# State-space stage of a two-block network: conditioning rows in one bank, another TensorE order, eight powers of C

## The reference

```python
def adaln(cond, w, b):
    return jnp.split(jax.nn.silu(cond) @ w + b, 6, axis=-1)
def s5_discretise(a_re, a_im, log_dt, b_re, b_im):
    lam = lax.complex(a_re, a_im); dt = jnp.exp(log_dt)[:, None]
    lam_bar = jnp.exp(lam * dt)
    b_bar = ((lam_bar - 1) / lam)[..., None] * b
    return lam_bar, b_bar
def s5_scan(u, lam_bar, b_bar, s0, reverse):
    bu = jnp.einsum('btgh,gph->btgp', u, b_bar)
    first = -1 if reverse else 0
    bu = bu.at[:, first].add(lam_bar * s0)
    a = jnp.broadcast_to(lam_bar, bu.shape)
    _, states = lax.associative_scan(_lin_rec_combine, (a, bu), axis=1, reverse=reverse)
    return states
def s5_mixer(...):
    y_lat = u_lat * d
    for direction in range(2):
        st_ctx = s5_scan(uc_ctx, lam_bar, b_bar, s0, reverse)
        s_ctx_final = st_ctx[:, 0] if reverse else st_ctx[:, -1]
        st_lat = s5_scan(uc_lat, lam_bar, b_bar, s_ctx_final, reverse)
        y_lat = y_lat + jnp.einsum('btgp,ghp->btgh', st_lat, c_mat).real
    z = gelu(y_lat); a, g = jnp.split(z @ w_glu, 2, axis=-1)
    return a * sigmoid(g)
```

## Time and profile before

| | us |
|---|---|
| median of 3 runs | 3676.69 (3676.04 to 3678.21) |
| profiled execution | 3674.07 |
| its span, first to last instruction | 3672.3 |
| PE busy | 3381.4 (92%) |
| DVE, ACT, POOL busy | 2140.5, 1399.7, 500.4 |
| granted clock, mean | 0.939 |
| HBM read | 637.54 MB, 175 GB/s over the span |

### The profile page before, as it was taken

One profiled execution on the slowest core, in us unless ns is written; L12 is line 12 of the kernel. 1 busy time (PEld: TensorE's weight loads), 2 busy tenths in 40 slices (PEclk: granted clock), 3 DMA queues, 4 the chain that ended last, 5 costly groups with the idle time before them and its releaser, 6 DMA issues.

```text
span 3672.3 us, 53215 instructions
## 1 busy us (share of the span) xinstructions
PE 3381.4 (92%) x21377; PEld 2858.0 (78%) x21377; DVE 2140.5 (58%) x1867; ACT 1399.7 (38%) x1409; POOL 500.4 (14%) x339
## 2 busy tenths in 40 slices
PE   3778888979999999897698999999999899999998
PEld 2456667868888888776577888888877788888887
DVE  6337665555565656659855555555563555555555
ACT  3245553443333333332234433433332344344333
POOL 1647780000000000029300000000000000000000
PEclk8678778989999999998889999999999999999999
DMA  7776666535556565443224555555542455555552
GB/s 224 248 258 202 202 207 217 187 96 183 185 181 194 185 192 183 160 138 134 101 94 148 186 191 184 186 190 184 187 153 80 143 189 188 183 189 185 193 183 92
DMA packets 350993, 642.91 MB, mean 175 GB/s; under 512 B 21599, under 2 KB 50359, under 8 KB 350519
## 3 DMA queue, kind: packets, MB, share of 16 engines
q1 hardware_dynamic: 350080, 641.37, 53.1%
q10 hardware_dynamic: 823, 0.29, 0.0%
HBM read 637.54 MB, written 4.06 MB: 175 GB/s over the span
## 4 chain that ended last, share of the span: by engine, by line
PE 86%; DVE 5%; ACT 3%; DMA 3%; issue 2%; DVEq 0%; ACTq 0%; SPq 0%
PE acc L436 48%; PE acc L437 24%; PE acc L1186 2%; ACT u L1435 2%; DMA raw<-in_w_mod_dram 2%; PE acc L1245 2%; PE acc L1216 1%; DVE z L912 1%; DVE w_lo L758 1%; PE acc L1292 1%; PE acc L1280 1%; PE acc L1262 1%; PE acc L1231 1%; PE acc L516 1%; PE acc L528 1%
## 5 line engine op out<-in xcount | busy, mean ns | idle before, releaser
L436 PE MATMUL acc<-xin,w_hi 128*128 128x512 f32 x5376 | 1912.1, 399 | 58.0 <-DVE xin L772 33.7
L758 DVE TENSOR_TENSOR w_lo<-raw,w_hi 128x2048 fp32r<-128x2048 f32 x488 | 1120.1, 2301 | 1079.3 <-ACT w_hi L612 1078.9
L437 PE MATMUL acc<-xin,w_lo 128*128 128x256 f32 x5376 | 1519.1, 283 | 0.0
L612 ACT ACTIVATE w_hi<-raw 128x2048 fp32r<-128x2048 f32 x488 | 934.3, 1918 | 1365.4 <-PE acc L437 1364.3
L436 PEld LDWEIGHTS acc<-xin,w_hi 128*128 128x128 f32 x5376 | 1017.5, 189 | 309.9 <-issue 35.9
L437 PEld LDWEIGHTS acc<-xin,w_lo 128*128 128x128 f32 x5376 | 1021.4, 190 | 0.0
L436 PE MATMUL acc<-hid,w_hi 128*128 128x512 f32 x2432 | 845.4, 392 | 0.0
L437 PE MATMUL acc<-hid,w_lo 128*128 128x256 f32 x2432 | 681.2, 280 | 0.0
L436 PEld LDWEIGHTS acc<-hid,w_hi 128*128 128x128 f32 x2432 | 455.1, 187 | 101.3
L437 PEld LDWEIGHTS acc<-hid,w_lo 128*128 128x128 f32 x2432 | 459.6, 189 | 0.0
L764 DVE TENSOR_REDUCE tmp<-acc 128x1024 f32<-128x2048 f32 x116 | 264.9, 2284 | 19.9 <-PE acc L437 19.9
(11 more groups left out here) (237 smaller groups left out, 2286.1 us busy)
## 6 DMA issues: line engine op xcount, KB each, us to landing
raw<-in_w_mod_dram SPq DMA_DIRECT2D x96, 1024.0 KB, 9.2
raw<-in_ffn_w_gate_dram SPq DMA_DIRECT2D x88, 1024.0 KB, 5.2
raw<-in_ffn_w_up_dram SPq DMA_DIRECT2D x88, 1024.0 KB, 5.2
raw<-in_ffn_w_down_dram SPq DMA_DIRECT2D x88, 1024.0 KB, 5.1
raw<-in_w_mlp_in_dram SPq DMA_DIRECT2D x64, 1024.0 KB, 5.3
raw<-in_w_mlp_out_dram SPq DMA_DIRECT2D x64, 1024.0 KB, 5.1
raw<-in_s_w_glu_dram SPq DMA_DIRECT2D x32, 1024.0 KB, 5.5
raw<-in_ab_w_in_dram SPq DMA_DIRECT2D x32, 1024.0 KB, 5.5
```

Source lines behind the costliest of these rows:

```text
L436: pe.matmul(bank, w_hi[:, slot, w], operand[:, kt, :], start=(kt == 0), stop=False)
L437: ins = pe.matmul(bank[:, 0:TOK], w_lo[:, slot, w], operand[:, kt, 0:TOK], start=False, stop=(kt == UK * units - 1))
L612: act.activation(w_hi[:, slot, :], raw[:, slot, :, :].rearrange("p k n -> p (k n)"), ACT.Copy).then_inc(hi_ready, 1)
L758: dve.tensor_tensor(w_lo[:, slot, :], raw[:, slot, :, :].rearrange("p k n -> p (k n)"), w_hi[:, slot, :].bitcast(F32), SUB).then_inc(lo_re ...
```

## The change

Six things, all in the state-space stage:
1. `cond` has 63 columns, all zero but 15 (c), 47 (c_ctx) and 48 (c). `ada_rows` takes a window of 32 columns of it, so that each block's rows land on partitions of their own within each quadrant of bank 0 and add up there over all blocks. The bank is copied five times in place of 24 (after two modulation blocks each, and at the end), and `mod_columns` and `ada_columns` take all rows of a copy at once. `ada` is made by one addition at the end.
2. The blocks come at other places (lists MOD and ADA): four blocks ahead of tile 0, one in step -1, two in each of steps 0 to 3, one in each of steps 4 to 14. The rows of a block of the list ADA are taken in two halves.
3. TensorE's, ScalarE's and SP's steps have another order. x is turned by transposes in place of products by a unit matrix. The e transposes alternate between banks 3 and 5. The lag products loop over the four quadrants innermost.
4. C is multiplied by powers 0 to 7 (L of them), B's powers go one up (1 to 8): the factor lambda moves from C to B.
5. Ahead of tile 0: the sines come before ScalarE's copies of B, the parameter rows are turned after the four selections of B, and the first half of x is squared after two of them.
6. The loop over tiles is written out on all engines. The dense layers wait for one signal of `ada` in place of sixteen.

```diff
-        cond = s5("cond", [P, KT, 32])
+        cond = s5("cond", [P, KT, 63])
-        cpow = [s5(f"cpow{i}", [P, 2, CB, POW * GRP]) for i in range(2)]
+        cpow = [s5(f"cpow{i}", [P, 2, CB, L * GRP]) for i in range(2)]
-        MOD = [(0, 1), (2, 3), (5, 6), (8, 9)]
+        MOD = [(0, 1), (2, 3), (6, 8), (10, 12)]
+        ADA = [4, 5, 7, 9, 11] + list(range(13, 24))
...
+            for n in range(KT + 1):
+                if n < KT:
+                    toeplitz(n, n % 2)
+                if n + 3 < KT:
+                    sp.wait_ge(c_sel, n + 3)
+                    load_c(n + 3)
+                    sp.wait_ge(xt_scaled, n + 3)
+                    load_x(n + 3)
+                if n + 1 < KT:
+                    ada_units(ADA[n + 1], (n + 1) * UN + 2 * D)
+                if n < 4:
+                    ada_units(MOD[2 + n // 2][n % 2], (1 - n % 2) * D + (2 + n // 2) * UN)
...
-            def ada_rows(m):
-                if not isinstance(m, int) or m > 0:
-                    pe.wait_ge(ada_sb, m)
-                for kk in range(UK):
+            def ada_rows(m, window, units=range(UK)):
+                for kk in units:
                     pe.wait_ge(raw_ready[kk], 16 * (m + 1))
                     for q in range(UK):
-                        ins = pe.matmul(ps[0][32 * q:32 * q + 32, :], cond[:, kk * UK + q, :], raw[:, kk, q, :],
-                                        start=(kk == 0), stop=(kk == UK - 1))
+                        ins = pe.matmul(ps[0][32 * q:32 * q + 32, :], cond[:, kk * UK + q, window:window + 32], raw[:, kk, q, :],
+                                        start=(m + kk == 0), stop=(kk == UK - 1), skip_group_check=True)
...
+                if n > 1:
+                    pe.wait_ge(y_gelu, n - 1)
                 for g in range(GT):
-                    ins = pe.matmul(ps[6][:, g * 64:(g + 1) * 64], xt[:, g, :, :].rearrange("c j h -> c (j h)"), ident[0:64, 0:64],
-                                    start=True, stop=True)
+                    ins = pe.transpose(ps[6][:, g * 64:(g + 1) * 64], xt[:, g, :, :].rearrange("c j h -> c (j h)"), ident[0:64, 0:64])
...
-                for kp in range(GT // 2):
-                    for d in range(2):
-                        win, to = ((0, 112), (GRP, 0))[d]
-                        for ri in range(2):
+                pe.wait_ge(e_sb, 4 * (n + 1))
+                for d in range(2):
+                    to = 7 * GRP * (1 - d)
+                    for ri in range(2):
+                        for kp in range(GT // 2):
                             ins = pe.matmul(ps[5][32 * kp:32 * kp + 32, to:to + P],
...
+            select_b(0)
+            select_b(1)
...
+            mod_rows(0, 0)
+            mod_rows(0, 1)
+            pe.wait_ge(b_sb, 4)
+            mod_columns(0)
+            select_c(0)
+            mod_rows(1, 0)
+            pe.wait_ge(c_sb, 1)
+            spread_modulation(0)
+            select_c(1)
+            transpose_x(0)
+            transpose_e(0, 0)
+            transpose_e(0, 1)
+            mod_rows(1, 1)
...
+                if 0 <= k < 4:
+                    mod_rows(2 + k // 2, k % 2)
...
+            act.wait_ge(angle_ready, 1)
+            act.activation(tv[4][:, :], tv[4][:, :], ACT.Sin)
+            act.activation(tv[5][:, :], tv[5][:, :], ACT.Sin).then_inc(sin_ready, 1)
...
             copy_b(0)
             copy_b(1)
-            act.wait_ge(angle_ready, 1)
-            act.activation(tv[4][:, :], tv[4][:, :], ACT.Sin)
-            act.activation(tv[5][:, :], tv[5][:, :], ACT.Sin).then_inc(sin_ready, 1)
-            copy_adarow(MOD[0][0])
+            square_x(0)
             copy_b(2)
             copy_b(3)
-            square_x(0)
...
             dve.reciprocal(rstd_x[:, :], rstd_x[:, :]).then_inc(rstd_ready, 1)
+            modulation(cm, 0)
...
-            pe.wait_ge(ada_done, KT)
+            pe.wait_ge(ada_done, 1)
```

More of the change, by code:

```diff
@@ L1221, in transpose_e @@
                 pe.wait_ge(bpow_done, n + 1)
-                pe.wait_ge(ada_sb, 2 if isinstance(n, int) and n == 0 else ada_block(n - 1) + 1)
-                for q in range(4):
-                    if q == 1:
+                for q in (2 * part, 2 * part + 1):
+                    if q == 0:
                         pe.wait_ge(mod_t, n + 1)
-                        pe.wait_ge(c_sb, n + 2 if upto(n, KT - 2) else KT)
+                        pe.wait_ge(c_sb, min(n + 2, KT))
                     if q >= 2:
@@ L1286, in output_transposes @@
                 pe.wait_ge(y_gelu, n + 1)
[L1287 to L1289 removed]
+                if n:
                     pe.wait_ge(z_lo, n)
@@ L1487, in _ @@
             copy_r8(0)
-            def tile(k, b):
-                before = isinstance(k, int) and k < 0
-                if not before:
-                    if upto(k, KT - 2):
+            copy_adarow(1, MOD[1][1])
+            for k in range(-1, KT):
+                if k >= 0:
+                    if k + 1 < KT:
                         act.wait_ge(s_done, k + 1)
@@ L1756, in _ @@
             powers_of_b(c0, 1)
-            first, steps, short = c0.n, 28, 17
             def rotate(c, k, b):
@@ L1793, in rotate @@
                 c.settle(1)
-                if not (isinstance(k, int) and k == 0):
+                if k:
                     dve.wait_ge(y_done, k)
@@ L1805, in rotate @@
                 ins.then_inc(s_done, 1)
-            def tile(k, b):
-                if isinstance(k, int) and k < 0:
-                    return
-                c = Chain(dve, dve_step, first + (k * steps if upto(k, KT - 2) else (KT - 2) * steps + short))
-                rotate(c, k, b)
-                if upto(k, KT - 2):
-                    copy_lags(c, k + 1)
-                if not (isinstance(k, int) and k == 0):
+            for k in range(KT):
+                rotate(c0, k, k % 2)
+                if k + 1 < KT:
+                    copy_lags(c0, k + 1)
+                if k:
                     finish(k - 1)
-                if isinstance(k, int) and k <= 2:
-                    modulation(cm, k + 1)
-                if upto(k, KT - 3):
+                if k in (0, 3, 5):
+                    modulation(cm, {0: 1, 3: 2, 5: 3}[k])
+                if k + 2 < KT:
                     dve.wait_ge(s_done, k + 1)
-                    powers_of_b(c, k + 2)
-                    assert c.n == steps, c.n
-                elif k == KT - 2:
-                    assert c.n == short, c.n
-            s5_pipeline(dve, tile)
+                    powers_of_b(c0, k + 2)
+                if k == KT - 1:
+                    dve.wait_ge(ada_col, 5)
+                    tt(ada[:, :].rearrange("p (n r) -> p n r", r=NT), ps[3][:, 0:4 * KT].rearrange("p (r n) -> p n r", r=NT),
+                       par[:, 0:4 * KT].rearrange("p (n r) -> p n r", r=NT), ADD).then_inc(ada_done, 1)
             finish(KT - 1)
```

365 lines of the change are left out of this document (160 added, 205 removed).

## The result

| | before | changed |
|---|---|---|
| median of 4 runs each (lowest to highest), us | 3676.4 (3672.6 to 3678.2) | 3636.7 (3631.3 to 3640.2) |
| ratio, 95% interval | | 0.9892 (0.9879 to 0.9904) |
| profiled execution; its span | 3674.07; 3672.3 | 3635.63; 3633.5 |
| first lag product | 96.8 | 86.1 |
| end of the state-space stage | 574.6 | 533.0 |

The change gains 1.1%, 40 us, where 87 were forecast: the direction was right, the size less than half, and the time lies 11 us above the range. All of it is in the stage. Behind it both traces have TensorE busy 2944 and 2946 us in 3096 us, at a clock of 0.97.

A forecast was written before the change was run, and what follows sets the result against it. A chain of waits through loads, TensorE and ScalarE bounds the state-space stage. Lead-in 78, first tile 17.5, four of 32, ten of 24.2, tail 22: 487.5 us against 574.6, so 3589 us; range 3562 to 3626.

The forecast's parts named there:

- Lag products, x, powers of C: Steady tile: lag products 1.2 us (before 3.92, 2.84), x transposes 1.0 (before 2.81), eight powers of C, worth nothing.
- The w_mod loads: Steady tile: block issued 4.3 us after the lag products start; new TensorE wait about 4 us, 2 more for unit 1.
- From there: Steady tile behind that wait: rows, spread, selection, x, u, e, output transposes; T of 23.6 to 24.2 us.
- T: Steady tile: time from one lag product's start (S) to the next; forecast 24.2 us, against 25.4 before.
- Rival 2: Tiles: TensorE's clock falls, the new wait may spread this; T gains 1.9 us, kernel 3622 us; chance 0.14.
- The transfer rate: Bursts of w_mod: kept the trace's 374 to 410 GB/s; by the skill's 358, T would be 24.7 us.
- Lead-in: Before the first lag product: forecast 78 us, ends 73 and 82, against 96.8 before; second x half landing at 44.2.
- Step -1: First tile, with one block: it waits for VectorE's powers of B, then e; forecast 17.5 us.
- Steps 0 to 3: The four tiles after the first, two w_mod blocks each: 32 us each, 128 in all.
- Rivals 1: Steady tiles: the block is in time, without the wait; T about 20 us, kernel 3547 us; chance 0.09.
- 3: Lead-in doesn't shrink: second x half lands late, first lag product stays at 97 us, kernel 3608 us; chance 0.05.
- Rival 4: Slower: unit 0 lands 12.5 us after issue in place of 5.5; T 31 us, kernel 3686 us; chance 0.04.

The follow-up runs named there:

- run 2: The changed kernel with x turned by products with the unit matrix in place of its 8 transposes a tile: 3683.1 us, ratio 1.0017 to the kernel before.
- run 5: The changed kernel with the w_mod block issued ahead of C and x, and x turned by products in place of transposes: 3619.1 us.
- run 6: Run 1 with the lag products in their old loop order: 3600.8 us.
- Run 1: The changed kernel with the late w_mod block issued right behind the lag matrices, ahead of C and x: 3594.8 us.
- Run 4: The changed kernel, block still late, with TensorE doing products of constants over the wait from step 4 on: 3610.0 us.
- run 8: Run 7 with GpSimd's scaling of the powers in three parts, tiles 2 and 3 first: 3590.7 us.
- run 3: The kernel before with C and x issued ahead of the w_mod block, nothing else: 3797.1 us, ratio 1.0327.
- run 7: The changed kernel with the block behind C and x in steps 0 to 3, but right behind the lag matrices from step 4 on: 3588.9 us.
- run 11: Run 7 with units 0 and 1 of the next block issued between writing and reading r_scratch from step 5 on: 3582.1 us.
- run 12: Run 11 with C and x also issued between writing and reading r_scratch in steps 0 to 4: 3582.8 us.
- run 9: The changed kernel with VectorE's six angle products put ahead of its wait for the square root in the lead-in: 3652.9 us.

## Why the prediction was wrong in size

- **Lag products, x, powers of C: right.** The group was forecast at 1.2 and takes 1.08 at the full clock; x at 1.0 takes 0.7 to 1.1. Runs 2, 5 and 6 give their worth: x as transposes is worth 46 us in this kernel, more than the 40 that the whole change gains over the kernel before, and 24 once the block is early; the loop order 2.2 us of TensorE a tile, of which little reaches the end once the block is early. GpSimd, which was said not to bound the tile, indeed did not (18.9 of 27.0); at tiles of 20 the longest waits are for it.
- **The w_mod loads: right**, place and length, to 0.5 us. Run 1 shows what the late block costs in all: 42 us. The forecast called it about 6 us a tile, most of the gain handed back.
- **"From there": the step that failed.** The rows of the block, the spread, the selection and the output transposes were costed at the durations that they have at the full clock, 5.6 us in all, though the step just above had put a standstill ahead of them. They take 9.7, TensorE ends at S+24.6 instead of S+21.1, and T is 27.4, not 24.2. x and e were sized rightly, by luck: their price was a reading at the lower clock, which the forecast did not notice. Run 4, with the same lateness and hardly a standstill, has tiles of 23.2 to 24.2. That this is the forecast's T is luck in part, too: there unit 0's rows start later than forecast (10.5 for 9.8), x is shorter (0.6 for 1.0) and the other rows are longer (2.6 for 1.8).
- **Rival 2 had the mechanism** ("the new wait may spread this") and gave it 0.14 and 3622. Its size came from a factor on the lag products, which in fact stay at the full clock, since the low stretch ends ahead of them; the pieces right behind the wait take up to twice as long. The prediction would have taken a clock below 0.7 over the tiles as a sign of being wrong; it was 0.75, and that was enough. Its sentence on the rule of the Trainium skill (TensorE: Matmul & The Clock Gate, Part 4), that transposes don't count as busy for the clock as other matmuls do, is not borne out here for x: with products the clock is 0.72, with transposes 0.75. Only the x transposes were exchanged; those of e stayed, and in run 4 the clock is down to 0.51 while they run. In the kernel before it fell in x's products, so transposes just ahead are not needed for it. The rule is open for e.
- **The transfer rate.** The bursts at the block are 377 to 394 GB/s again, above the 358 of the Trainium skill (DMA: Bandwidth & Descriptors, Specifications). Keeping the trace's rate was right.
- **Lead-in, forecast 78, measured 86.1.** Its top end was 82, and beyond 85 was named as a sign of being wrong. VectorE waited for the squares until 57.4, 5.4 later than forecast, because the second half of x landed at 49.7 instead of 44.2: the DMA engines are busy 0.99 of the lead-in at 294 GB/s, and x shares them with w_mod. The chain that ended last does not go over x at all but over the first two blocks, which were not in the sum: TensorE waits for the last unit of the first until 36.9, for that of the second until 60.3. By then the squares, though late, were done.

```profile
14.52 22.36 DMA raw<-in_w_mod_dram
...
43.73 16.54 DMA raw<-in_w_mod_dram
```

- **Step -1, 22.9 for 17.5.** GpSimd's phases of tile 0 waited for the angles until 89.0. The angles' products, 1.7 us before, took 7.5 beside GpSimd's powers of C, and no term had that.
- **Steps 0 to 3, 130.7 for 128:** right as a sum, and in part by luck. The forecast had 32 for each; they take 26.8 to 39.3. Within them step 0 is GpSimd's scaling of 14 tiles (12.5 us), which the forecast did not have, and the others are SyncE's chain. That nothing is left of GpSimd's 7.4 us is run 8.
- **Rivals 1, 3 and 4** did not happen. Rival 4's threshold, unit 0 12 us after its issue, was not reached: 5.3. But run 3 shows that its sign was a real danger for this order of loads; the new TensorE order is, as I read it, what keeps it off.
- **The rest** was carried over and differs by 2.8 us (3100.5 from the stage's end to the span's end, before 3097.7).

What stays open: why steps 2 to 4 stay at 28 to 40 us in runs 7, 8, 11 and 12, and with tile 6 at 273 to 275 each time, whatever GpSimd or C and x do. Their chain is shown, a kernel that shortens its long members (the write of r_scratch, the block) was not run. Nor was an experiment made that takes GpSimd away from VectorE's products in the lead-in; the cause stands on three places of one operation and on its 128 x 8 neighbour. And open is what makes the clock fall where TensorE is at work (run 4 at 405 us, the kernel before at 340).

## What to carry to other kernels

A wait that an edit adds to TensorE has two prices, the time that it stands and what everything right behind it costs at the lower clock; here the first was forecast and the second was the miss, and filling the wait with useless products took 27 us off the kernel. When loads change places in one queue, follow the ring: what lets the queue pass, what it issues late, who waits for that, and whether this leads back to the start. And test each part of a bundled change alone: here one part (x) was worth 46 us, and another, in the same diff, cost 42.

## What the runs showed of the hardware that was not expected

- The granted clock fell from 1.00 to 0.60 and 0.50 right behind a standstill of TensorE of 3.4 us with a second of 1.6, and was at 0.75 on average over the tiles; with products in the standstill it was 0.95. It also fell to 0.51 with TensorE at work, at 405 us of run 4.
- VectorE's products of 128x128 took 0.2 to 0.3 us each with GpSimd at rest and 1.1 to 2.2 with its products of 128x1024 beside them; one of 128x8 took 1.72 in run 9, beside a product of GpSimd of 1.92.
- In the lead-in, with w_mod, x and C in the queues together, the core moved 294 GB/s at a DMA share of 0.99; in the bursts of w_mod of a steady tile 377 to 394.
